# Moving row transposes into other weight units of a two-layer block kernel

## The reference

```python
# first block
merged = (s_gla * (y_gla @ w_gla_out) + s_dsa * (y_dsa @ w_dsa_out)
          + s_mem * (y_mem @ w_x_out))
x = x + rmsnorm(merged @ w_o, g_post)
# second block
#   y_gdn: gated delta rule, rms-normed per head, times silu(z)
#   y_nsa: 8 query heads in 2 groups; compressed keys (15 blocks), selected keys and
#          a window, three softmaxes, each weighted by its gate
#   gated sum of y_gdn @ w_branch_gdn and y_nsa @ w_branch_nsa, times w_out, added to x
#   then a gated feed-forward of width 2816, and rms_norm(x, final_norm_gain)
```

## Time and profile before

| | us |
|---|---|
| median of 3 runs | 912.6 (912.44 to 913.03) |
| the profiled execution | 912.57 |
| its span | 910.8 |
| TensorE busy | 888.0 |
| VectorE busy | 567.8 |
| ScalarE busy | 437.8 |
| GpSimd busy | 52.8 |

### The profile page before, as it was taken

How to read it: one execution, slowest core, us unless ns; L and a number is a source line. 1 busy time by engine, 2 the same in 40 slices (tenths; PEclk the granted TensorE clock), 3 DMA queues, 4 the chain that set the end, 5 groups by cost and what they waited for, 6 DMA issues and landing times.

```text
span 910.8 us, 14487 instructions
## 1 busy us (share of the span) xinstructions
PE 888.0 (97%) x5984; PEld 776.8 (85%) x5984; DVE 567.8 (62%) x856; ACT 437.8 (48%) x632; POOL 52.8 (6%) x79
## 2 busy tenths in 40 slices
PE   7999999999999999999999999999999999999997
PEld 5999999899999888888779999677877788888885
DVE  4955564573657665655569878754376677777544
ACT  6744444744344544444356514753434455555441
POOL 1000000000030110000020141000000000000000
PEclk9999999999999999999999999999999999999999
DMA  9657744455455545555667665004664565655441
GB/s 297 222 185 216 225 140 138 139 185 184 125 156 184 184 145 180 164 195 188 215 188 160 166 138 188 1 3 139 139 231 151 171 188 188 187 186 193 170 162 46
DMA packets 127799, 151.71 MB, mean 167 GB/s; under 512 B 16967, under 2 KB 93126, under 8 KB 127734
## 3 DMA queue, kind: packets, MB, share of 16 engines
q1 hardware_dynamic: 127594, 150.70, 53.3%
q0 software_dynamic: 64, 0.07, 0.0%
q10 hardware_dynamic: 76, 0.02, 0.0%
HBM read 148.67 MB, written 3.68 MB: 167 GB/s over the span
## 4 chain that ended last, share of the span: by engine, by line
PE 88%; DVE 6%; ACT 2%; DMA 1%; issue 1%; SPq 1%; POOL 0%; POOLq 0%; DVEq 0%; ACTq 0%
PE bank L511 21%; PE bank L513 20%; PE bank L512 20%; PE bank L1217 9%; PE bank L1205 5%; DVE w_lo L1907 2%; DVE arena L2268 1%; DMA arena<-in_mem 1%; PE bank L790 1%; PE bank L915 1%; PE bank L691 1%; PE bank L671 1%; PE bank L1029 1%; PE bank L1010 1%; ACT w_hi L1393 1%
## 5 line engine op out<-in xcount | busy, mean ns | idle before, releaser
L1907 DVE TENSOR_TENSOR w_lo<-ring,w_hi 128x2048 fp32r<-128x2048 f32 (+1 forms) x134 | 301.0, 2251 | 176.3 <-ACT w_hi L1393 175.8
L1393 ACT ACTIVATE w_hi<-ring 128x2048 fp32r<-128x2048 f32 (+1 forms) x134 | 250.2, 1870 | 124.0 <-PE bank L513 83.4
L511 PE MATMUL bank<-h_both,w_hi 128*128 128x256 f32 x624 | 179.3, 287 | 1.7 <-DVE w_lo L1907 1.7
L512 PE MATMUL bank<-h_both,w_hi 128*128 128x256 f32 x624 | 176.5, 283 | 0.0
L513 PE MATMUL bank<-h_both,w_lo 128*128 128x256 f32 x624 | 176.5, 283 | 0.0
L1217 PE MATMUL bank<-h_both,w_hi 128*128 128x512 f32 x352 | 123.4, 398 | 0.0
L511 PEld LDWEIGHTS bank<-h_both,w_hi 128*128 128x128 f32 x624 | 119.6, 192 | 3.8 <-DVE w_lo L1907 2.3
L512 PEld LDWEIGHTS bank<-h_both,w_hi 128*128 128x128 f32 x624 | 119.7, 192 | 0.6 <-issue 0.5
L513 PEld LDWEIGHTS bank<-h_both,w_lo 128*128 128x128 f32 x624 | 119.7, 192 | 0.0
L1205 PE MATMUL bank<-h_both,w_lo 128*128 128x256 f32 x352 | 97.8, 281 | 0.4 <-ACT h_both L1416 0.4
L1408 ACT ACTIVATE arena<-bank 128x512 f32<-128x512 f32 (+5 forms) x91 | 45.5, 522 | 100.3 <-PE bank L513 87.3
(11 more groups left out here) (332 smaller groups left out, 1362.4 us busy)
## 6 DMA issues: line engine op xcount, KB each, us to landing
ring<-in_w_in SPq DMA_DIRECT2D x59, 1024.0 KB, 5.2
ring<-in_w_gate_up SPq DMA_DIRECT2D x44, 512.0 KB, 4.6
ring<-in_w_down SPq DMA_DIRECT2D x10, 1024.0 KB, 5.0
ring<-in_w_mem_kv SPq DMA_DIRECT2D x8, 1024.0 KB, 7.1
ring<-in_w_in SPq DMA_DIRECT2D x8, 512.0 KB, 4.9
ring<-in_w_gla_out SPq DMA_DIRECT2D x4, 1024.0 KB, 5.0
ring<-in_w_x_out SPq DMA_DIRECT2D x4, 1024.0 KB, 5.1
ring<-in_w_dsa_out SPq DMA_DIRECT2D x4, 1024.0 KB, 5.7
```

The source lines that it names most:

```text
L511: mm(o, ah, bh, start=start, stop=False, skip_group_check=True)
L512: mm(o, ah, bl, start=False, stop=False, skip_group_check=True)
L1393: act(w_hi[:, k % NHI, 0:m], ring[:, order.index(name) % NSLOT, 0:m], ACT.Copy)\
L1907: tt_(w_lo[:, i, 0:m], ring[:, i, 0:m], w_hi[:, k % NHI, 0:m].bitcast(F), ALU.subtract)\
```

## The change

Five edits. (1) The DMA of the identity goes to ScalarE's queue, as its first. (2) A new `rows_projection` opens four banks and runs unit a of column half 0, then the transposes of the last two column pairs, then unit a of half 1, unit b of half 0, unit b of half 1; both merges use it, and the weights are loaded in that order. (3) The compressed transposes move behind the logits of step 3, with a wait for the copy of cp3 before the compressed part of no0; ScalarE's copies move behind its exponentials 6 and 7. (4) The gt transposes go between the token tiles of bn1, T20 and T21 between those of bg1, T22 and T23 between w2o0a and w2o1a; VectorE's order follows. (5) The last quarter of the result is scaled by ScalarE and stored from its queue.

```diff
@@ TensorE
+            def rows_projection(name, x, tag, last_rows):
+                for c in range(2):
+                    for t in range(TT):
+                        open_bank(f"{name}{c}{t}")
+                tokens_part(f"{name}0", f"{name}0a", x, 0, 4, KT - 1, tag)
+                last_rows()
+                tokens_part(f"{name}1", f"{name}1a", x, 0, 4, KT - 1)
+                tokens_part(f"{name}0", f"{name}0b", x, 4, 8, KT - 1, tag)
+                tokens_part(f"{name}1", f"{name}1b", x, 4, 8, KT - 1)
...
-            def rest_of_rows():
-                transpose_wide("1", merged, (2, 3))
-                pe.wait_ge(*read("T13"))
-
-            wide_tokens("wo0", (mg_hi, mg_lo), rest_of_rows, tag="1")
-            wide_tokens("wo1", (mg_hi, mg_lo))
+            rows_projection("wo", (mg_hi, mg_lo), "1", lambda: transpose_wide("1", merged, (2, 3)))
...
+                if r == 0:
+                    pe.wait_ge(*read("cp3"))
                 for g in range(2):
                     ins = mm(outs[g], vcn[0:15, 64 * g:64 * g + 64], pcT[0:15, ...
...
                 if i % 2 == 1 and i + 4 < 16:
                     nsa_logits((i + 3) // 2)
+                if i == 3:
+                    compressed_transposes()
                 if i % 4 == 3:
                     nsa_out(i // 4)
...
             level_end(2)
-            compressed_transposes()
             nsa_step(3)
...
             merge_part("bn", 0, (oT_hi, oT_lo))
-            merge_part("bn", 1, (oT_hi, oT_lo))
-            pe.wait_ge(*read("gd1"))
-            for j in range(2):
-                bank = open_bank(f"gt{j}")
-                ...
+            merge_part("bn", 1, (oT_hi, oT_lo), None, gdn_transposes)
             merge_part("bg", 0, (z2_hi, z2_lo), "z2_split")
-            merge_part("bg", 1, (z2_hi, z2_lo))
-            transpose_wide("2", ma, range(4))
-            wide_tokens("w2o0", (m2_hi, m2_lo), tag="2")
-            wide_tokens("w2o1", (m2_hi, m2_lo))
+            merge_part("bg", 1, (z2_hi, z2_lo), None, lambda: transpose_wide("2", ma, (0, 1)))
+            rows_projection("w2o", (m2_hi, m2_lo), "2", lambda: transpose_wide("2", ma, (2, 3)))
@@ SP and ScalarE
-            sp.dma_start(ident, consts[:, 0:128]).then_inc(signal("ident_in"), 16)
+            sc.dma_start(ident, consts[:, 0:128]).then_inc(signal("ident_in"), 16)
...
                     causal_exp("n", i + 4)
+                if i == 3:
+                    compressed_copies()
...
-            compressed_copies()
             nsa_step(3)
...
             for t in range(TT):
-                for c in range(2):
+                for c in range(2 - t):
                     sp.wait_ge(signal("result"), 2 * t + c + 1)
...
+            sc.wait_ge(signal("last_product"), 1)
+            sc.wait_ge(signal("rstd_o"), 2)
+            last = xn[:, 1, 512:1024]
+            act(last, last, ACT.Copy, scale=rstd[:, 3:4]).then_inc(signal("last_result"), 1)
+            sc.wait_ge(signal("last_result"), 1)
+            sc.dma_start(out[0, 128:256, 512:1024], last).then_inc(signal("out_done"), 16)
@@ VectorE, second merge (order; bodies unchanged)
+            nsa_branch(0, 0); nsa_branch(0, 1); nsa_branch(1, 0)
             # gt0, gt1 into z2; low parts of z2
+            nsa_branch(1, 1)
+            gdn_branch(0, 0); gdn_branch(0, 1); gdn_branch(1, 0)
+            low_of_rows("2", m2_lo, m2_hi, (0, 1))
+            gdn_branch(1, 1)
+            lows(splits_by["T21"] + 2)
+            low_of_rows("2", m2_lo, m2_hi, (2, 3))
             lows(splits_by["T23"] + 2)
-            low_of_rows("2", m2_lo, m2_hi, range(4))
```

More of the change, by code:

```diff
@@ L554, in project_tokens, with tokens_part @@
                 unit_used[name] = full(name)
-            def tokens_part(title, unit_name, x, k0, k1, last, tag=None, pair_ready=None):
+            def tokens_part(title, unit_name, x, k0, k1, last, tag=None, pair_ready=None, between=None):
                 wh, wl = split_unit(unit_name, 512)
@@ L573, in tokens_part @@
                         part_done(unit_name, ins)
+                    if between is not None and t == 0:
+                        between()
+            def rows_projection(name, x, tag, last_rows):
[7 more added lines that the diff above has]
+                tokens_part(f"{name}1", f"{name}1b", x, 4, 8, KT - 1)
             def wide_tokens(title, x, between=None, tag=None):
@@ L2490, in _, with nsa_branch @@
                 tt_(gd_rows[:, s, :], by_head(f"gd{t}"), rb, ALU.mult).then_inc(reader(f"gd{t}"), 1)
-            for c in range(2):
-                for t in range(TT):
-                    title = f"bn{c}{t}"
-                    v = mb[:, t, 512 * c:512 * c + 512]
-                    bank_ready(title)
-                    stt(v, v, 1.0, bank_of(title)[:, :], ALU.add, ALU.mult).then_inc(reader(title), 1)
+            def nsa_branch(c, t):
+                title = f"bn{c}{t}"
+                v = mb[:, t, 512 * c:512 * c + 512]
+                bank_ready(title)
+                stt(v, v, 1.0, bank_of(title)[:, :], ALU.add, ALU.mult).then_inc(reader(title), 1)
+            nsa_branch(0, 0)
+            nsa_branch(0, 1)
+            nsa_branch(1, 0)
             for j in range(2):
@@ L2503, in _, with gdn_branch @@
                 tt_(pair(z2_lo, j), pair(z2, j), pair(z2_hi, j).bitcast(F), ALU.subtract).then_inc(signal("z2_split"), 1)
-            for c in range(2):
-                for t in range(TT):
-                    title = f"bg{c}{t}"
-                    v = ma[:, t, 512 * c:512 * c + 512]
-                    bank_ready(title)
-                    stt(v, v, 1.0, bank_of(title)[:, :], ALU.add, ALU.mult).then_inc(reader(title), 1)
-                    ve.wait_ge(*read(title))
-                    ins = tt_(v, v, mb[:, t, 512 * c:512 * c + 512], ALU.add)
-                    if t == 0:
-                        step(ins)
-                    else:
-                        ins.then_inc(signal("rows_2"), 1)
+            nsa_branch(1, 1)
+            ve.wait_ge(*read("bn11"))
+            def gdn_branch(c, t):
+                title = f"bg{c}{t}"
+                v = ma[:, t, 512 * c:512 * c + 512]
+                bank_ready(title)
+                stt(v, v, 1.0, bank_of(title)[:, :], ALU.add, ALU.mult).then_inc(reader(title), 1)
+                ve.wait_ge(*read(title))
+                ins = tt_(v, v, mb[:, t, 512 * c:512 * c + 512], ALU.add)
+                if t == 0:
+                    step(ins)
+                else:
+                    ins.then_inc(signal("rows_2"), 1)
+            gdn_branch(0, 0)
+            gdn_branch(0, 1)
+            gdn_branch(1, 0)
+            low_of_rows("2", m2_lo, m2_hi, (0, 1))
+            gdn_branch(1, 1)
+            lows(splits_by["T21"] + 2)
+            low_of_rows("2", m2_lo, m2_hi, (2, 3))
             lows(splits_by["T23"] + 2)
-            low_of_rows("2", m2_lo, m2_hi, range(4))
             ve.wait_ge(signal("x_mid_back"), 16)
@@ L2570, in _ @@
                     ve.wait_ge(*read(f"wd{c}{t}"))
-                    step(tt_(xn[:, t, s], v, g_fin[:, s], ALU.mult))
+                    ins = tt_(xn[:, t, s], v, g_fin[:, s], ALU.mult)
+                    if (c, t) == (1, 1):
+                        ins.then_inc(signal("last_product"), 1)
+                    else:
+                        step(ins)
             for t in range(TT):
```

18 lines of the change are left out of this document (11 added, 7 removed).

## The result

The changed kernel takes 914.16 us (median of 20 runs, 911.26 to 915.96), the kernel before beside it 912.04 us (20 runs). The ratio is 1.0025, 95% interval 1.0018 to 1.0031: about 2.3 us slower, where 1.0 us faster was forecast. One later run of the kernel before, 981.07 us at a mean clock of 0.848, is a slow one and is left out of every number. The profiled execution of the changed kernel took 914.35 us with a span of 912.6; its mean granted clock was 0.991, before 0.997.

The account below looks back on a forecast made before the run. TensorE, busy 888.0 of 910.8 us, was taken to bound the kernel, so only its idle and low-clock time could be won. Terms -0.1 - 1.3 + 0.9 + 0.9 - 1.2 - 0.2 = -1.0 gave 911.6 us, range 909.8 to 913.2.

Parts of the forecast that it names:

- Start: Program start: identity DMA on ScalarE's queue lets SP's later issues come sooner; -0.1 us.
- First merge: First block's merge: wo1a covers the idle 1.57 us, part given back at the phase's end; -1.3 us.
- Compressed transposes: Compressed attention: ScalarE's copies queue behind exponentials 6 and 7, so no0's compressed part waits for cp3; +0.9 us.
- Clock: Behind the cp3 wait: idle TensorE brings the clock down and dense level 3 pays; +0.9 us, bounds 0 and 1.7.
- Second merge: Second merge: bg0 starts sooner and the 0.84 us wait goes, part given back at the end; -1.2 us.
- At its end 0.8 is given back: End of the second merge: w2o01's sum and square delay the last square, returning 0.8 of TensorE's 2.0 us lead.
- End: Program end: ScalarE scales and stores the last quarter, ready and issued sooner; -0.2 us.
- D: Rival, chance 0.18: low clock lasts into levels 3 and 4; two periods give 913.6, or 914.5 us.
- B: Rival, chance 0.24: around the cp3 wait the clock stays up or falls within the wait only; 910.7 us.
- C: Rival, chance 0.08: the cp3 wait does not bind, copies coming before the exponentials in effect; 907.0 us.

Follow-up runs that it names:

- e15: Changed kernel with identity products filling three waits: before cp3 and at both phase ends; 911.53 us, ratio 1.0000.
- e16: Kernel before with identity products filling its three longer waits: first phase end, compressed probabilities, bg0; 910.67 us, ratio 0.9985.
- e6: Changed kernel with three identity products in front of the wait for cp3; 911.72 us, ratio 1.0004.
- e7: Changed kernel with more identity products at both phase ends (six instead of four, four instead of two); 913.54 us, ratio 1.0022.
- e8: Changed kernel with VectorE's sum of w2o10 moved before the low part of gu0b; 911.97 us, ratio 1.0007.
- e14: Kernel before with the fifth edit alone; run once for its profile, time not used; 6.9 us from last matmul to end of span.
- e13: Kernel before with the first edit alone; run once for its profile, time not used; 7.6 us from last matmul to end of span.
- e10: Changed kernel, but SP issues the last quarter's store after ScalarE scales it; profile only, time not used; 7.4 us from last matmul to end.
- e5: Changed kernel with ScalarE's four compressed copies moved before exponentials 6 and 7; 908.56 us, ratio 0.9965.
- e11: Kernel before with two identity products ahead of its wait for the compressed probabilities; 912.24 us, ratio 0.9997.
- e12: Changed kernel with the repairs of e5 and e8, fifth edit undone, six identity products instead of four at the first phase end; 906.78 us, ratio 0.9944.

## Why the prediction was wrong

The forecast said -1.0 us, and between the two profiled executions the span grew by 1.8. The 2.8 us between them, term by term: start 0.0, first merge +0.45, wait for cp3 -0.3, clock +0.5, second merge +1.5, end +0.7. The steps that failed are what stands at the end of the second merge, the clock (priced at one place, too low, and against a row that already had it), and the end of the program. A kernel slower by more than 1.8 us had been given a chance of 0.04.

**Start, -0.1:** the -0.12 of the table proves nothing, since T12 of different executions lies 1.5 us apart with and without the edit; e15 less e16 gives -0.01. The price of the edit lay at the other end of the program, +0.5, and no step of mine looked there.

**First merge, -1.3:** the profile shows -0.85, the filled kernels -1.1. The order on ScalarE and VectorE came as written. Mis-sized is what is late next: TensorE gained 1.85 us (1.7 forecast), and 0.7 of it went back into the wait at the phase end, which grew to 2.03 us (0.4 forecast); the clock fell behind it, another 0.25 (29.65 us from T12 to c0, in e6, e7 and e8 29.40).

**Compressed transposes, +0.9 of waiting:** the mechanism was right instruction for instruction (0.77 idle, exponentials, copies, 3.35 idle), and against the profiled execution the term was +0.57. But its reference was a row at the lower clock. I had the earlier trace rows in hand and said that the level cost 1.4 to 1.7 "inside the time before", and did not ask whether other executions have it. Against those that don't, the wait costs 2.2. In edit 3 alone, with the clock low for twice as long, the whole term is +4.5, where +1.8 was forecast: over the runs of an edit by itself this is the largest miss.

**Clock, +0.9:** it was +1.4 to +1.5. I let part of the period fall into the wait; it fell wholly on the work behind it. The Trainium skill (TensorE: Matmul & The Clock Gate, "Why this matters for your kernels") warns that the clock goes back to its lower level after long idle gaps between bursts of matmuls. It spoke for the larger value and was right here: 5 of 5 profiles behind 3.35 us. But its rule is for gaps longer than the 2.11 us of the earlier trace rows, which I counted as agreeing with it; falls behind waits of 2.0 to 2.1 us (13 of 28) go beyond it. The gaps of the earlier trace rows, which I set against it, "did no harm" in that execution; behind the wait of the earlier trace rows the clock fell in one of eight profiles.

**Second merge, -1.2:** it was +0.26 between the two profiles, and there this is the step that failed most. Up to w2o0a every time was met within 0.3 us, and TensorE was 1.8 us ahead. "At its end 0.8 is given back" should have been 1.2, since both last sums wait behind VectorE's low part, which itself waits for ScalarE's high part, and three short waits became one of 2.11 us; and then 0.9 more for the clock behind it. Without that fall, at full clock, the merge gains 0.7, and over its runs the edit alone gained 0.8 (0.0 to 1.6). I asked for the clock at one place of the program and nowhere else.

**End, -0.2:** for the fifth edit nearly right (e14: -0.1). The +0.5 measured comes from the first edit (e13).

**Rivals.** D had the sign and the size (913.6 to 914.5), but in the changed kernel's profile not the mechanism: each low stretch stayed as short as in the earlier trace rows, and there were three that cost time, at 459, 582 and 718. In the profiles of edit 3 alone and of e10 the clock was low for 6.8 us, twice as long, which is nearer to D. B fell. C did not happen by itself, but e5 shows that its mechanism was there to be had: with the copies in effect before the exponentials, the kernel gains 5.5 us over the changed one.

**Left open.** What decides in which execution a wait of about 2 us is followed by the lower clock; why e7 gained less in its median than in its profile; what the idle piece at 32.6 us in e11 and e12 waits for, and in how many executions it stands.

## What to carry to other kernels

When a wait is moved on one engine, move its partner on the other engine to the same place in the order: transposes behind logits are good only if their copies don't stand behind exponentials. Read a phase end as a chain of its own, and ask what each queue converts ahead of the last sums. Before taking a row of the profile as the base of a sum, look whether its slice was at full clock; and where idle TensorE time is gathered into one piece, price the clock at every such place.

## What the hardware showed that was not expected

- The clock can fall after TensorE has resumed (wait up to 580.2, low from 582), so the wait of 3.35 us costs 1.5 us more than itself. In two other profiles (edit 3 alone, e10) it fell inside that wait and stayed low for 6.8 us, and the work behind it up to ma0 took 2.4 us more instead of 1.4.
- Identity products in a wait kept the clock up: it was low behind none of the 11 filled waits of the table, and behind 19 of the 41 left as they are. The 11 runs of e16 lie within 0.43 us, where those of the kernel before spread over 4.
- One DMA fewer in SP's program moves an instruction packet into the last stores, which then land in 2.6 us instead of 2.2.
- A store of 256 KB takes nearly the same from SP's queue (2.9 us) and from ScalarE's (3.0 to 3.2, once 2.8) when it is the last of four and that packet is among them; without it 2.4 from SP's and 2.5 from ScalarE's.
